# A Trainium2 transformer block in fp32: PSUM as four pairs of banks in the FFN output stage, and what is laid out anew around it

## What is computed

```python
h2 = rms_norm(x, norm2_w[l]) * (1.0 + scale2) + shift2
g, u = jnp.split(h2 @ w_ffn_in[l], 2, axis=-1)
x = x + gate2 * ((jax.nn.silu(g) * u) @ w_ffn_out[l])
```

## Time and profile before

| | |
|---|---|
| median of three runs | 2728.28 us (2724.64 to 2728.41) |
| the profiled execution's own time | 2726.23 us |
| its span, first to last instruction | 2724.6 us |
| PE busy | 2631.8 us, 97% |
| mean granted TensorE clock | 0.985 of full speed |
| the FFN output stage | from 2197.6 us to the end |

### The profile page before, as it was taken

The page is one execution under the profiler, slowest core; times in us unless marked ns, Lnnn a source line. Parts: engine busy times, 40 slices in busy tenths (PEclk is TensorE's granted clock), DMA queues, the critical chain, the costliest instruction groups (busy, mean ns, idle before and its releaser), DMA issues.

```text
span 2724.6 us, 40311 instructions
## 1 busy us (share of the span) xinstructions
PE 2631.8 (97%) x15228; PEld 2312.6 (85%) x15228; DVE 1936.7 (71%) x2798; ACT 1056.9 (39%) x1411; POOL 277.6 (10%) x275
## 2 busy tenths in 40 slices
PE   7999999999999999999999999999999979899897
PEld 6777888888888888888899999999999967777676
DVE  6878888833333477654678889888888866577667
ACT  5443333433333322222554444444444433333332
POOL 0000100100000111232000000000000010001134
PEclk9999999999999999999999999999999989999999
DMA  9967676533333477776344454454445584656752
GB/s 360 307 188 219 182 207 178 159 101 98 98 101 93 140 248 237 229 236 200 90 149 136 158 163 134 157 163 147 144 156 165 184 311 155 239 205 213 262 177 85
DMA packets 387002, 488.48 MB, mean 179 GB/s; under 512 B 19236, under 2 KB 314424, under 8 KB 386200
## 3 DMA queue, kind: packets, MB, share of 16 engines
q1 hardware_dynamic: 346896, 348.80, 40.9%
q0 software_dynamic: 34304, 131.48, 13.8%
q10 hardware_dynamic: 5640, 5.89, 0.6%
HBM read 416.37 MB, written 69.74 MB: 178 GB/s over the span
## 4 chain that ended last, share of the span: by engine, by line
PE 82%; DMA 6%; DVE 5%; issue 2%; ACT 1%; POOL 1%; SPq 1%; DVEq 0%; POOLq 0%; ACTq 0%
PE bank L784 12%; PE bank L786 12%; PE bank L785 12%; PE bank L1111 10%; PE bank L1114 10%; PE bank L1113 10%; PE bank L1177 3%; PE bank L1178 3%; PE bank L1179 3%; PE bank L865 2%; DMA ww<-in_w_ffn_out 2%; DMA y_tm<-y_t 1%; PE bank L949 1%; DVE lo_ring L2107 1%; DMA mov<-u_fm 1%
## 5 line engine op out<-in xcount | busy, mean ns | idle before, releaser
L1111 PE MATMUL bank<-mov,w_slot 128*128 128x256 f32 x2240 | 632.0, 282 | 0.8 <-ACT blocks L1530 0.8
L1114 PE MATMUL bank<-mov,w_slot 128*128 128x256 f32 x2240 | 631.6, 282 | 0.0
L1113 PE MATMUL bank<-mov,w_slot 128*128 128x256 f32 x2240 | 631.5, 282 | 0.0
L784 PE MATMUL bank<-h_hi,w_hi 128*128 128x512 f32 x1248 | 492.7, 395 | 0.0
L786 PE MATMUL bank<-h_hi,w_lo 128*128 128x512 f32 x1248 | 486.9, 390 | 0.0
L785 PE MATMUL bank<-h_lo,w_hi 128*128 128x512 f32 x1248 | 485.9, 389 | 0.0
L1659 DVE TENSOR_TENSOR w_lo<-w_raw,w_hi 128x1024 fp32r<-128x1024 f32 x188 | 233.6, 1243 | 304.9 <-ACT w_hi L1197 304.5
L1111 PEld LDWEIGHTS bank<-mov,w_slot 128*128 128x128 f32 x2240 | 426.9, 191 | 1.1 <-ACT blocks L1530 1.0
L1113 PEld LDWEIGHTS bank<-mov,w_slot 128*128 128x128 f32 x2240 | 427.2, 191 | 0.0
L1114 PEld LDWEIGHTS bank<-mov,w_slot 128*128 128x128 f32 x2240 | 426.9, 191 | 0.0
L1197 ACT ACTIVATE w_hi<-w_raw 128x1024 fp32r<-128x1024 f32 x188 | 199.0, 1060 | 487.7 <-PE bank L786 380.3
(11 more groups left out here) (296 smaller groups left out, 3915.4 us busy)
## 6 DMA issues: line engine op xcount, KB each, us to landing
w_raw<-in_w_ffn_in SPq DMA_DIRECT2D x352, 256.0 KB, 3.1
w_raw<-in_w_ada SPq DMA_DIRECT2D x128, 512.0 KB
u_fm<-u_stage POOLq DMA_DIRECT2D x22, 1792.0 KB, 8.4
w_raw<-in_w_in SPq DMA_DIRECT2D x128, 256.0 KB
w_raw<-in_w_in SPq DMA_DIRECT2D x60, 512.0 KB
ramp_w<-in_w_ada SPq DMA_DIRECT2D x24, 1024.0 KB, 13.0
w_raw<-in_w_out SPq DMA_DIRECT2D x32, 512.0 KB
mov<-u_fm POOLq DMA_DIRECT2D x7, 2048.0 KB, 10.6
```

Source lines behind the costliest of these rows:

```text
L784: nc.tensor.matmul(bank[b][:], lhsT=whi[:, cols], rhs=xh, start=first_k, stop=False)
L1111: nc.tensor.matmul(dst, lhsT=wh, rhs=xh, start=s == 0 and t == 0, stop=False, skip_group_check=True)
L1113: nc.tensor.matmul(dst, lhsT=wh, rhs=xl, start=False, stop=False, skip_group_check=True)
L1114: mm = nc.tensor.matmul(dst, lhsT=wl, rhs=xh, start=False, stop=last, skip_group_check=True)
```

## The change

PSUM is declared as four tensors of two neighbouring banks, each product of the stage is put in one of them, and one instruction of 1024 columns reads both banks. The same edit also

- takes the chunks in sizes 6, 8, 8 in place of 8, 8, 6, so that the groups have 3, 3, 4, 4, 4, 4 steps;
- swaps products 3 and 5 (b22 comes before b21), drops `ww`, and loads b21 into `zw` once b22's low part is made; the next b22 waits for `form_n`;
- brings only pieces 1, 3, 5 of six column blocks back at first, and the others by `load_mov` after product 0, two of them ahead of the last `store_u`;
- gives the results fixed places (`y_slot`), two of them used by turns;
- moves multiplication by gate2 and the sum with x from POOL to DVE (`gate_2`, `add_residual`), reads the turned x from PSUM without a copy, and moves its loads from POOL's queue to ACT's (`load_residual`), with one buffer `x2f`; the four transposes of a group come before products 3, 4, 6 and the next product 0 (for the last group, before the last step).

```diff
-CHUNKS = (8, 8, 6)
+CHUNKS = (6, 8, 8)
...
-PRODUCTS = ((1, "b11", "a"), (3, "t", "c"), (5, "r", "a"), (2, "b21", "b"), (4, "q", "a"), (6, "b22", "c"), (0, "n", "a"))
...
+PRODUCTS = ((1, "b11", "a"), (3, "t", "c"), (5, "r", "a"), (6, "b22", "c"), (4, "q", "a"), (2, "b21", "b"), (0, "n", "a"))
...
+ADDED = {0: Y11, 1: Y22, 2: Y12, 3: Y12, 4: Y22, 5: Y11, 6: Y21}
...
+        yw = [at(f"yw{d}", FORGET + (4 + 2 * d) * T if d < 3 else STORE + 24 * T, 2 * S) for d in range(4)]
+        zw = [at(f"zw{d}", WHI + 2 * d * T if d < 3 else STORE + 26 * T, 2 * S) for d in range(4)]
...
+        x2f = at("x2f", STORE + 32 * T, 2 * S)
+        g2b = [at(f"g2b{d}", STORE + (34 + d) * T, S) for d in range(2)]
+        scaled = yw[0]
...
+        banks_2 = [ctx.enter_context(nc.psum_tensor(f"banks{b}", [P, 2 * S], F32)) for b in range(4)]
+        bank = [banks_2[b // 2][:, b % 2 * S:(b % 2 + 1) * S] for b in range(8)]
...
-        PAIR_A, PAIR_B, PAIR_C = ((7, 0), (3, 2)), (5, 1), (6, 4)
...
+        PAIR_A, PAIR_B, PAIR_C = ((6, 7), (2, 3)), (4, 5), (0, 1)
...
+        def both(banks):
+            return banks_2[banks[0] // 2][:]
...
+        def turns(i, idx, d):
+            if i == NG - 1 and (idx, d) == (6, GROUPS[i][3] - 1):
+                return [(i, Y21)]
+            if d:
+                return []
+            if i == NG - 1 and idx == 0:
+                return [(i - 1, Y21)]
+            return [(i, e) for e, at_ in ((Y12, 3), (Y22, 4), (Y11, 6)) if idx == at_]
...
+            def load_b21(i):
+                for d in range(GROUPS[i][3]):
+                    sp.wait_ge(lo_p, NV + step_no(i, 3, d) + 1)
+                    load_w(i, d, 1, 0, zw[d], x_landed[d])
...
+            sp.wait_ge(e_unit, NV - 1)
+            for d in range(GROUPS[0][3]):
                 load_w(0, d, 0, 1, yw[d], raw_landed[d])
-            for d in range(4):
-                if d == 2:
+            sp.wait_ge(e_unit, NV)
+            for d in range(GROUPS[0][3]):
+                load_w(0, d, 1, 1, zw[d], x_landed[d])
+            load_b21(0)
+            for i in range(1, NG):
+                new = range(GROUPS[i - 1][3], GROUPS[i][3])
+                if new:
                     sp.wait_ge(u_ready, FG)
-                load_w(0, d, 1, 1, zw[d], x_landed[d])
-            load_b21(0, 0)
...
+                for d in range(GROUPS[i][3]):
+                    if d not in new:
+                        sp.wait_ge(lo_p, NV + step_no(i - 1, 4, d) + 1)
+                    load_w(i, d, 0, 1, yw[d], raw_landed[d])
+                for d in range(GROUPS[i][3]):
+                    if d not in new:
+                        sp.wait_ge(*formed(i - 1, "n", d))
+                    load_w(i, d, 1, 1, zw[d], x_landed[d])
+                for d in range(GROUPS[i][3]):
+                    if d not in new:
+                        sp.wait_ge(lo_p, NV + step_no(i - 1, 6, d) + 1)
+                    load_w(i, d, 0, 0, xw[d], e_raw[d])
+                load_b21(i)
...
-                if idx in (2, 4, 5, 6):
-                    pe.wait_ge(*evicted(i, {2: 0, 4: 2, 5: 1, 6: 4}[idx]))
+                if idx in (2, 3, 4, 6):
...
-                    pe.wait_ge(*evicted(i - 1, {1: 5, 3: 3}[idx]))
+                    pe.wait_ge(*evicted(i - 1, {1: 3, 5: 5}[idx]))
+                    if idx == 5 and GROUPS[i][0] == LAST_C:
+                        pe.wait_ge(gated, gated_no(i, Y12))
...
                     if i == NG - 1:
-                        pe.wait_ge(xt_copied, 2 * TB + 4)
+                        pe.wait_ge(gated, gated_no(i - 1, Y11))
...
+                return PAIR_B if e in (Y12, Y21) else PAIR_A[(i + 1) % 2]
...
+                if e == Y12:
+                    pe.wait_ge(*evicted(i - 1, 5))
+                    if i > NG - OG:
+                        pe.wait_ge(gated, gated_no(i - 1, Y21))
+                elif e == Y22:
                     pe.wait_ge(*evicted(i - 1, 6))
+                elif e == Y11:
+                    pe.wait_ge(gated, gated_no(i, Y22))
                 else:
-                    pe.wait_ge(xt_copied, 2 * TB + m)
-                pe.wait_ge(xr_landed[m % 2], 16 * (D_I + m // 2 + 1))
+                    pe.wait_ge(*evicted(i, 5))
+                pe.wait_ge(*residual_got(i, e))
...
-                    if c == LAST_C and 2 <= idx < 6:
-                        turn_residual(i, idx - 2)
+                    if c > 0 and n == 0 or i == 0 and idx >= 3:
+                        pe.wait_ge(mov_landed[idx], 16 * (c + (2 if 3 <= idx < CHUNKS[0] else 1)))
...
-                if r >= 3:
-                    act.wait_ge(y_stored[r % 3], 16 * (r // 3))
-                elif r:
+                if i:
+                    act.wait_ge(*y_free(i, ADDED[idx]))
+                elif idx:
                     act.wait_ge(u_stored, 16 * FG)
-                for t in range(2):
-                    nc.scalar.activation(tile(y_t[r % 3], t), bank[pair(i, PRODUCTS[idx][2])[t]][:], ACT.Copy
-                                         ).then_inc(ev_act, 1)
...
+                nc.scalar.activation(y_at(i, ADDED[idx])[:], both(pair(i, PRODUCTS[idx][2])), ACT.Copy).then_inc(ev_act, 1)
...
+            def load_residual(i, e):
+                n = gated_no(i, e)
+                if n == 1:
+                    act.wait_ge(u_stored, 16 * FG)
+                else:
+                    act.wait_ge(x_turned, 4 * TB + n - 1)
+                k0 = (GROUPS[i][1] * 2 + Y_COLS[e]) * 4
+                act.dma_start(x2f[:].rearrange("p (k n) -> p k n", k=4),
+                              y_fm[k0:k0 + 4, :, TOKENS[e] * P:TOKENS[e] * P + HB].rearrange("k p n -> p k n")
+                              ).then_inc(residual_got(i, e)[0], 16)
...
+                if i == NG - OG and idx == 0 and d == 0:
+                    load_residual(i, Y12)
+                if GROUPS[i][0] == LAST_C and d == GROUPS[i][3] - 1:
+                    for j, e in turns(i, idx, 0):
+                        n = gated_no(j, e)
+                        if n < 4 * OG:
+                            load_residual(NG - OG + n // 4, (Y12, Y22, Y11, Y21)[n % 4])
...
             def form_n(i, d):
-                dve.wait_ge(lo_p, NV + step_no(i, 3, d) + 1)
-                v.tensor_tensor(xw[d][:], ww[(S_BASE[i] + d) % 2][:], xw[d][:], ALU.subtract).then_inc(sums_done, 1)
+                dve.wait_ge(lo_p, NV + step_no(i, 5, d) + 1)
+                v.tensor_tensor(xw[d][:], zw[d][:], xw[d][:], ALU.subtract).then_inc(sums_done, 1)
...
+                if idx in (3, 4, 5):
+                    dve.wait_ge(*evicted(i, {3: 2, 4: 1, 5: 0}[idx]))
+                elif c:
+                    dve.wait_ge(*y_got(i, e))
                 else:
-                    dve.wait_ge(*evicted(i, e))
+                    dve.wait_ge(*y_free(i, e))
+                y, src = y_at(i, e)[:], both(pair(i, PRODUCTS[idx][2]))
+                if c == 0 and idx == 6:
+                    v.tensor_copy(y, src).then_inc(ev_dve, 1)
+                else:
+                    v.tensor_tensor(y, src, y, ALU.add).then_inc(ev_dve, 1)
...
+            def gate_2(i, e):
+                if (i, e) == (NG - 1, Y21):
+                    dve.wait_ge(*y_got(i, e))
+                else:
+                    dve.wait_ge(*evicted(i, LAST_OF[e]))
...
+                v.tensor_tensor(two(y_at(i, e)), two(y_at(i, e)), g2b[Y_COLS[e]][:, None, :].to_broadcast([P, 2, S]),
+                                ALU.mult).then_inc(gate_mul, 1)
...
+            def add_residual(i, e):
+                dve.wait_ge(gate_mul, gated_no(i, e))
+                dve.wait_ge(x_turned, 4 * TB + gated_no(i, e))
+                turned_2 = both(PAIR_B if e in (Y12, Y21) else PAIR_A[(i + 1) % 2])
+                v.tensor_tensor(y_at(i, e)[:], turned_2, y_at(i, e)[:], ALU.add).then_inc(gated, 1)
+            def add_last():
+                i = NG - 1
+                add_residual(i, Y11)
+                gate_2(i, Y21)
+                add_residual(i, Y21)
+                dve.wait_ge(e_unit, NV + done_no(i, 6))
...
+                if q == RING2:
+                    form_t(0, 0)
                 if q >= RING2:
                     low_2(q)
                 if q == RING2:
+                    form_t(0, 1)
                     u_product(FG - 1)
-                    form_t(0, 0)
-                    form_t(0, 1)
...
-                if idx == 3 and d:
+                if idx == 5 and d:
                     form_n(i, d - 1)
-                if idx == 4 and d == 0:
+                if idx == 6 and d == 0:
                     form_n(i, last_d)
-                if d == 2 and (idx or i):
-                    add_y(*((i, idx - 1) if idx else (i - 1, 6)))
+                j, before = (i, idx - 1) if idx else (i - 1, 6)
+                if d == 2 and j >= 0:
+                    add_y(j, before)
+                if j >= 0 and GROUPS[j][0] == LAST_C and before >= 3 and d == last_d:
+                    gate_2(j, ADDED[before])
```

(53 more changed lines are left out.)

219 lines of the change are left out of this document (64 added, 155 removed).

## The result

The changed kernel takes 2657.6 us (median of four runs, 2656.4 to 2658.1) beside 2726.9 us for the kernel before on the same chip: ratio 0.9746, 95% interval 0.9729 to 0.9763. The profiled execution takes 2658.1 us, its span 2656.5 us. 2656.6 us were forecast.

The account below looks back on a forecast made before the run. PE, busy for 97% of the span, bounds the kernel; only its stalls can be won. Remaining terms sum to 29.6 us in place of 101.3, 71.7 less: 2728.28 - 71.7 = 2656.6 us, range 2643 to 2677.

Parts of the forecast that it names:

- The wide reads: 1024-column PSUM reads on DVE and ACT, taken at 1.2 and 1.06 us: 0 us on the path.
- The start: First steps of the output stage: old stalls go, step 9 waits for the last `u_stage` store; 8.5 us remain (5 to 18).
- b21 in `zw`: Four windows where ACT waited for `ww`: b21 loaded earlier into `zw` removes 35.7 us, lower clock included.
- Group 1 to 2: Change of group: PE waits 2.7 us for `xw`, plus 1.8 us of lower clock: 4.5 us (0 to 10).
- Group 3 to 4: Change of group with four steps: `xw` comes almost in time, 0.5 us lost (0 to 3).
- 11.6 us are there and 11.5 needed: Time available against time needed for `xw` at the change from group 3 to 4, hence 0.5 us.
- The last chunk: Groups 4 and 5: transposes 7.0 us, waits for the sum before product 6 1.4, x loads 1.0.
- the 15.4 us before the first x: Old window at 2576.6, 11.6 us of it idle for the first `x2f`; loading x 12 steps ahead removes it.
- The tail: After PE's last matmul: DVE 2.4, store 2.1, then 2.2 to the span's end: 6.7 us (5.5 to 8) for 12.2.
- transfers set the start and the change of chunk: Rival, chance 0.19: the start's store takes 19.0 us and SP's loads in group 1 cost 10 us: 2672 us.

Follow-up runs that it names:

- the chunks' run: The changed kernel with chunk sizes 8, 8, 6 as before, and the first `yw` and `zw` loads placed as before: 2654.9 us, ratio 0.9730.
- the run with late pieces: The changed kernel with the next chunk's pieces of products 4, 5, 6 loaded only in the next group: 2651.3 us, ratio 0.9722.
- the run with the sum made early: The changed kernel with next `xw` loads ahead of the last `zw`, pieces 4 to 6 loaded next group, `add_residual` right behind `gate_2`: 2648.9 us, 0.9714.

## Why the prediction came out right, and which terms were off

The total was off by 1 us; its terms were off by up to 5, in both directions: 32.5 us of excess in place of 29.6 in the trace, and the profiled execution at 2658.1 in place of 2654.5. What brought the median of 2657.6 within 1 us of the forecast is that the forecast was put 2.05 us above the profiled execution, and the changed kernel's median is 0.5 below its own. That the total came out within 1 us is luck: the terms' errors nearly cancel. The mechanisms were forecast rightly, but for one change of group that was taken as all but hidden.

- **The wide reads, 0 us.** Shown by two runs. Taken at 1.2 and 1.06 us; measured 1.216 and 1.012.
- **The start, 8.5 forecast, 5.7 measured.** The chain is the one forecast, and its times from PE's start are close: step 7 at 21.9 (22.4), the store landed at 27.1 (27.9), step 9 at 30.6 (31.3). What was wrong is the 2 us of lower clock added to it. PE did run 2.1 us slow in that window, but in the steps before 9, while it had to wait for the store anyway; step 9 itself ran at full clock. The store took 8.36 us, the median, not 8.8: the loads ahead of it had all but landed (the second at 2218.3, 1.2 us after its issue). With four loads behind it in its queue the store took 8.7 us. The Trainium skill (DMA: Bandwidth & Descriptors, Queues, rings and completion order) has each DMA engine take a queue's descriptors in order, so that what is issued behind a transfer isn't taken up ahead of it; the trace agrees. In the chunks' run the store was issued 10 us ahead of the landing of an earlier load of its queue and took 16.1 us; that fits a delay by what lies ahead, but transfers of SP ran beside it too.
- **b21 in `zw`, 35.7 us.** Shown: the waits are gone, and with them back 63 us return, 41 of them at b21 itself, where the earlier trace rows had 35.7 and about 3. The other 22 are nearly all at the changes of group, where the kernel before lost nothing, so 63 us is the price of this wait in the new layout and not what its removal won.
- **Group 1 to 2, 4.5 forecast, 7.3 measured.** PE was idle 4.2 us (15.6 less 11.4) in place of 2.7. The load took 10.4 us, as forecast. But `xw` went out 2.1 us behind the `low_2` that freed it, not 1.15: two `zw` of the new fourth step's group stand ahead of it in SP's queue, and that `low_2` was itself 0.6 us late, behind `form_n` and `add_y` on DVE: 10.4 + 2.1 + 0.6 less 8.8 is 4.3 us. The lower clock cost 3.1 us (11.4 busy for 8.3 of work) in place of 1.8.
- **Group 3 to 4, 0.5 forecast, 5.7 measured.** This is the step that failed: "11.6 us are there and 11.5 needed" took 10.3 us for the load of `xw`, from one row, and it took 13.8 us. The 2 MB pieces are not the difference between the two, for one ran beside the row's load as well. DMA issues of the kernel before from 2376 to 2390 us:

```profile
xw<-in_w_ffn_out SPq DMA_DIRECT2D x4, 512.0 KB, 9.1
mov<-u_fm POOLq DMA_DIRECT2D x1, 2048.0 KB, 13.4
```

At the change from group 1 to 2 the first `xw` took 10.4 us with pieces of that size too, the other three 13.8 to 14.7. So 13.8 us is within what such a load takes in this traffic, and one row didn't show it. Without the pieces beside it the same load takes 7.8 us (the run with late pieces). Why it took 13.8 us here and 10.3 there stays open. A forecast with a margin of 0.1 us had no right to its upper bound of 3.
- **The last chunk, 9.4 forecast, 8.7 measured.** PE's waits for the sum before product 6 are the 0.7 us each that were forecast, as the run with the sum made early shows (4.3 less 3.5 and 3.6). The x loads cost nothing where 1.0 was taken. That the 15.4 us before the first x are gone, as forecast, is read from the trace alone, and so is what the tail won: no run takes either back.
- **The tail, 6.7 forecast, 5.1 measured.** DVE's 2.5 us were right. The store and what follows took 2.6, not 4.3: the 2.2 us behind the landing in the earlier trace rows don't come back.

Of the rivals, "transfers set the start and the change of chunk" was half true: the changes of chunk were set by transfers (13.0 us in place of 5.0), while the store at the start took its median of 8.4 us and not 19.0. That POOL slows DVE is shown by the run with gate2 on POOL, at 3.43 us for 1.22. The Trainium skill (SBUF — State Buffer, Who interferes with whom) says that a DVE instruction with two SBUF inputs contends with a GpSimd one that reads SBUF; the trace agrees.

## What to carry to other kernels

Look at what an edit lays out anew before you price its title: here the title was worth nothing, and putting one wait on a buffer back cost 63 us. Price a wait in a queue with everything behind it. Where a transfer's landing and the need for it differ by tenths of a microsecond, take the bound from the longest such transfer that the trace has in like traffic, not from one row. Freeing an engine earlier also issues its transfers earlier, so the load that PE needs next must be put ahead of them.
